# Thirty-six projection columns in pairs of seven block products, with the weight sums made by accumulating transfers

## What is computed

```python
proj = jnp.einsum("bld,de->ble", h, w_in)
conv_in, z_c, u_s, z_s, g_c, g_s = jnp.split(proj, IN_OFFSETS, axis=-1)
ca, cb = jnp.split(conv_in, 2, axis=-1)
cu = causal_depthwise_conv(ca * jax.nn.sigmoid(cb), conv_w, conv_b)      # 31 taps
cu = jax.nn.silu(layer_norm(cu, conv_ln_g, conv_ln_b))
conv_out = jnp.einsum("blc,cd->bld", cu * jax.nn.silu(z_c), w_conv_out)
y = jax.nn.gelu(s5_mimo(u_s, ...))
y = y * jax.nn.sigmoid(jnp.einsum("blc,ce->ble", y, w_glu) + b_glu)
ssm_out = jnp.einsum("blc,cd->bld", y * jax.nn.silu(z_s), w_ssm_out)
merged = jax.nn.sigmoid(g_c) * conv_out + jax.nn.sigmoid(g_s) * ssm_out
out = jnp.einsum("bld,de->ble", merged, w_out)
```

## Time and profile before

| | us |
|---|---|
| median of 3 runs | 2224.04 (2223.0 to 2225.08) |
| profiled execution, its own time | 2223.35 |
| its span, first to last instruction | 2221.6 |
| outside the span | 1.75 |
| granted TensorE clock, mean | 0.994 |

### The profile page before, as it was taken

How to read it: one execution, slowest core, us unless ns; L and a number is a source line. 1 busy time by engine, 2 the same in 40 slices (tenths; PEclk the granted TensorE clock), 3 DMA queues, 4 the chain that set the end, 5 groups by cost and what they waited for, 6 DMA issues and landing times. The chain is left out here.

```text
span 2221.6 us, 20647 instructions
## 1 busy us (share of the span) xinstructions
PE 2144.1 (97%) x7074; PEld 1093.5 (49%) x7074; DVE 1319.3 (59%) x1860; ACT 596.5 (27%) x972; POOL 185.2 (8%) x140
## 2 busy tenths in 40 slices
PE   6999999999999999998999999999999999999998
PEld 5444444445655655655454455544444444444443
DVE  4787733364674674664723695377468888335533
ACT  4355522233333433433213320021100000221011
POOL 0000000121212302301100000000000000003200
PEclk8999999999999999999999999999999999999999
DMA  9333330121111111111410334321111110113021
GB/s 331 116 110 118 118 123 0 76 65 38 35 30 43 35 26 47 35 25 48 125 31 19 124 66 68 87 63 33 43 33 43 38 33 24 52 48 123 19 95 57
DMA packets 200911, 146.86 MB, mean 66 GB/s; under 512 B 49997, under 2 KB 171906, under 8 KB 200834
## 3 DMA queue, kind: packets, MB, share of 16 engines
q1 hardware_dynamic: 184305, 143.09, 21.5%
q10 hardware_dynamic: 16160, 1.90, 0.8%
q0 software_dynamic: 384, 1.05, 0.2%
HBM read 126.45 MB, written 18.38 MB: 65 GB/s over the span
## 5 line engine op out<-in xcount | busy, mean ns | idle before, releaser
L2150 PE MATMUL bank<-hT,ring 128*128 128x512 f32 x1472 | 635.6, 593 | 0.0
L2150 PEld LDWEIGHTS bank<-hT,ring 128*128 128x128 f32 x1472 | 279.7, 190 | 348.6 <-issue 348.3
L1238 PE MATMUL bank<-hT,ring 128*128 128x512 f32 x336 | 157.8, 596 | 1.8 <-ACT silu_z L1474 1.8
L2870 DVE SCALAR_TENSOR_TENSOR yT<-s_arena,yT 128x1024 f32<-128x1024 f32 x120 | 153.3, 1278 | 0.0
L2870 DVE SCALAR_TENSOR_TENSOR s_arena<-s_arena 128x1024 f32<-128x1024 f32 x112 | 143.1, 1278 | 0.0
L1828 DVE SCALAR_TENSOR_TENSOR memory<-memory,col_exp_last,bank 128x128 f32<-128x128 f32 x64 | 22.2, 348 | 153.8 <-PE bank L1418 153.8
L2150 PE MATMUL bank<-ssm_y,ring 128*128 128x512 f32 x192 | 83.9, 593 | 0.0
L1238 PEld LDWEIGHTS bank<-hT,ring 128*128 128x128 f32 x336 | 58.5, 191 | 49.8 <-issue 49.4
L1238 PE MATMUL bank<-resid,yT 128*128 128x512 f32 x168 | 82.5, 594 | 0.0
L2853 DVE TENSOR_TENSOR s_arena<-bank,s_arena 128x1024 f32<-128x1024 f32 x8 | 9.8, 1224 | 108.7 <-ACT s_arena L2489 108.7
L2489 ACT ACTIVATE s_arena<-bank 128x1024 f32<-128x1024 f32 x8 | 8.2, 1024 | 242.5 <-PE bank L2150 242.5
(11 more groups left out here) (559 smaller groups left out, 3446.3 us busy)
## 6 DMA issues: line engine op xcount, KB each, us to landing
ring<-in_w_in SPq DMA_DIRECT2D x48, 512.0 KB, 3.8
ada<-in_ada_w SPq DMA_DIRECT2D x8, 2048.0 KB, 8.3
ring<-in_gdn_in_w SPq DMA_DIRECT2D x32, 512.0 KB, 4.1
resid<-in_x SPq DMA_DIRECT2D x8, 1024.0 KB, 8.8
ring<-in_lru_in_w SPq DMA_DIRECT2D x16, 512.0 KB, 3.9
lru_arena<-in_ada_w SPq DMA_DIRECT2D x6, 1024.0 KB, 13.0
x_scratch<-resid SPq DMA_DIRECT2D x2, 2048.0 KB, 10.6
decayT<-g_scratch SPq DMA_DIRECT2D x8, 512.0 KB, 4.3
```

The source lines that it names most:

```text
L1238: last = nc.tensor.matmul(bank[:, to, :], w[:, k, :], v[:, k, :], start=(first and k == 0), stop=(k == KB - 1), skip_group_check=not only)
L2150: last = nc.tensor.matmul(bank[:, 2 * PAIR[name] + h, :], w[:, k, :], src[:, k, h * HALF:(h + 1) * HALF], start=(k == 0), stop=(k == kt - 1))
L2870: dve_b.mark(dve.scalar_tensor_tensor(out=acc, in0=padded[:, p, j:j + S], scalar=taps[:, p, j:j + 1], in1=acc, op0=ALU.mult, op1=ALU.add), ...
```

## The change

The 36 columns a, b (16), zs (4), gs (8) and gc (8) of w_in are now computed two at a time, in 18 pairs: `ab0`..`ab7` join a{n} with b{n}, `zs0`, `zs1`, `gs0`..`gs3` and `gc0`..`gc3` join column n of a group with the one half a group further. For a pair, the weights form 2 x 2 blocks (512 input features by one column) and h forms 2 x 2 blocks `h11 h12 h21 h22` (512 features by 512 positions). Seven products P1..P7 of four source products each replace eight. Four sums of h (`h_T1`..`h_T4`) are made once by VectorE; for each pair, four sums of weights `U1`..`U4` are read from DRAM. Those sums are made during the first block on POOL's queue: a plain copy DRAM to DRAM, then accumulating transfers onto it. `silu_zc` no longer stays in `resid`, since `h_T1`..`h_T3` take its place: ACT stores each column to DRAM, and POOL loads it back later. `zc6` and `zc7` move ahead, around `y1`. The order of ACT and VectorE after `y1` is written out anew.

POOL, in the first block (ab sums are 2 MB each, gs and gc 1 MB, zs 0.5 MB):

```diff
+                    def copy_U(group, u):
+                        block = {"U1": (1, 0), "U2": (0, 0), "U3": (0, 0), "U4": (0, 1)}[u]
+                        g.dma_start(w_sums[group, u], w_block(group, *block)).then_inc(U_copied[group], 16)
+                    def add_U1_U3(group):
+                        g.wait_ge(U_copied[group], 4 * 16)
+                        g.dma_start(w_sums[group, "U1"], w_block(group, 1, 1), accum_op=ALU.add, max_dma_last_dim=4096).then_inc(U13_summed[group], 16)
+                        g.dma_start(w_sums[group, "U3"], w_block(group, 1, 0), accum_op=ALU.add, max_dma_last_dim=4096).then_inc(U13_summed[group], 16)
+                    def add_U2(group):
+                        g.wait_ge(U13_summed[group], 2 * 16)
+                        g.dma_start(w_sums[group, "U2"], w_sums[group, "U1"], accum_op=ALU.add, ...).then_inc(U2_summed[group], 16)
+                    def add_U4(group):
+                        g.wait_ge(U2_summed[group], 16)
+                        g.dma_start(w_sums[group, "U4"], w_sums[group, "U2"], accum_op=ALU.add, ...).then_inc(U4_summed[group], 16)
                     for n in range(KT):
                         if n >= 2:
                             pe_a.wait(g, f"gates{n - 2}")
                         g.dma_start(gw[:, n % 2, :, :], ...).then_inc(gw_loaded[n % 2], 16)
+                        # n = 2: copy ab U1, U2; 3: copy ab U3, U4; 4: add_U1_U3(ab); 5: add_U2(ab), copy gs U1, U2; 6: add_U4(ab), copy gs U3, U4
+                    add_U1_U3("gs")
+                    for u in ("U1", "U2", "U3", "U4"):
+                        copy_U("zs", u)
+                    add_U2("gs")
+                    add_U1_U3("zs")
+                    for u in ("U1", "U2", "U3", "U4"):
+                        copy_U("gc", u)
+                    add_U4("gs")
+                    add_U2("zs")
+                    add_U1_U3("gc")
+                    add_U4("zs")
+                    add_U2("gc")
+                    add_U4("gc")
```

```diff
+            PAIR_ORDER = ["ab0", "ab1", "zs0", "ab2", "zs1", "ab3", "ab4", "ab5", "gs0", "ab6", "gs1", "ab7", "gs2", "gs3", "gc0", "gc1", "gc2", "gc3"]
+            PAIR_BANKS = {name: ((0, 1, 6), (2, 3, 7))[n % 2] for n, name in enumerate(PAIR_ORDER)}
+            SINGLE_AFTER = {"ab3": ["glu0", "glu1", "glu2", "glu3"], "gs0": ["ssm0"], "ab6": ["ssm4"], "ab7": ["ssm1"], "gs2": ["ssm5"],
+                            "gs3": ["ssm2", "ssm6", "ssm3", "ssm7"]}
...
+                    def product(name, q, start, alone, src):
+                        block_done(f"{name}_{q}")
+                        for k in range(HK):
+                            last = nc.tensor.matmul(bank[:, to, :], w[:, k, :], src[:, k, :], start=(start and k == 0), stop=(k == HK - 1), ...)
+                    # a pair: P1 h11, P5 h_T1, wait kept0, P6 h_T2, P2 h21, wait kept1, P7 h_T3, wait kept2, P3 h22, wait kept3, P4 h_T4
...
                     finish(early("zc5"))
-                    finish(early("zs0"))
+                    finish(early("zc6"))
                     dve_b.wait(pe, "s1")
                     read_out(1)
+                    finish(early("zc7"))
...
                         act_b.mark(act.activation(silu_zc[:, n, :], pair(PAIR[f"zc{n}"]), ACT.Silu), f"zc{n}")
+                        act_b.wait(act, f"zc{n}")
+                        act.dma_start(zc_dram[n], silu_zc[:, n, :]).then_inc(zc_kept if n < 6 else zc_kept_late, 16)
...
+                    for group in W_GROUPS:
+                        sp.wait_ge(U4_summed[group], 16)
+                    for x in W_BLOCKS[8:]:
+                        pe_b.wait(sp, W_AT[x][2])        # the block eight places earlier has been used
+                        load_block(x)
+                    for n in (3, 0, 1, 2):
                         load(f"co{n}", a["w_conv_out_2"][0], n)
```

```diff
+                    dve.wait_ge(zc_kept, 6 * 16)
+                    # h_T1 = h11 - h12, h_T3 = h22 - h12, h_T2 = -h_T1 - h22, after zc7 on PE: h_T4 = -h_T2 - h21 (each 128 x 2048)
+                    def join_quarter(name, which, to, kept, product):
+                        dve_b.mark(TT_(place, other, place, ALU.add), f"{name}_" + ("C11", "C12", None, "C22")[which])
+                    join_columns("ab0")
...
+                    # col 0: taps 1-15, join ab1, taps 16-30          col 1: taps 1-3, join zs0, taps 4-23, join ab2, rest
+                    # col 2: taps 1-8, join zs1, taps 9-27, join ab3  col 3: taps; then glu 0-3 and z 0-3
+                    # join ab4; col 4: taps 1-14, join ab5, rest      col 5: 1-2, join gs0, 3-8, merge 0, 9-26, join ab6, rest
+                    # col 6: 1, merge 4, 2-16, join gs1, rest         join ab7; col 7: 1-5, merge 1, 6-24, join gs2, rest; merge 5, join gs3
...
+                    pe_b.wait(g, "ssm7")
+                    dve_b.wait(g, f"sq_total{KT - 1}")
+                    for k in range(KT):
+                        if k >= 5:
+                            dve_b.wait(g, f"y{k - 5}")
+                        g.dma_start(zc_places[k % 5], zc_dram[k]).then_inc(zc_back[k % 5], 16)
```

More of the change, by code:

```diff
@@ L1945, in block_program @@
             SLOT = {}
-            for names, slot in (
-                (["u0", "zc0", "zc2", "zc4", "zs0", "zs2", "zc6", "b2", "a3", "a4", "a5", "a6", "a7", "gc0", "gc4", "co0", "co4"], 0),
-                (["u1", "zc1", "zc3", "zc5", "zs1", "zs3", "a2"] + [f"ssm{n}" for n in range(KT)] + ["gc1", "gc5", "co1", "co5"], 1),
-                (["u2", "a0", "a1", "glu0", "glu2", "zc7", "b3", "b4", "b5", "b6", "b7", "gc2", "gc6", "co2", "co6"], 2),
-                (["u3", "b0", "b1", "glu1", "glu3"] + [f"gs{n}" for n in range(KT)] + ["gc3", "gc7", "co3", "co7"], 3),
-            ):
+            for names, slot in ((["u0", "zc0", "zc2", "zc4", "zc6", "co0", "co4"], 0), (["u1", "zc1", "zc3", "zc5", "zc7", "co1", "co5"], 1),
+                                (["u2", "co2", "co6"], 2), (["u3", "co3", "co7"], 3)):
                 for n, name in enumerate(names):
                     SLOT[name] = (slot, q0 + n + 1, names[n - 1] if n else None)
+            for n in range(4):
+                SLOT[f"co{n}"] = SLOT[f"co{n}"][:2] + (LAST_IN_SLOT[n],)
             for n, freed in enumerate(("co_P3_0", "co_P4_0", "co_P3_1", "co_P4_1")):
@@ L1962, in co_weights @@
                         "S2": co_S2, "S3": co_S3, "S4": co_S4}
-            QUICK = (["zs0", "b0", "zs1", "zs2", "b1", "zs3", "zc6"] + [f"glu{b}" for b in range(ST)] + ["b2", "zc7", "gs0", "ssm0"]
-                     + [f"{x}{n + d}" for n in range(3, KT) for x, d in (("b", 0), ("gs", -2), ("ssm", -2))]
-                     + [f"{x}{n}" for n in (KT - 2, KT - 1) for x in ("gs", "ssm")] + [f"gc{n}" for n in range(KT)])
-            EARLY = [f"u{b}" for b in range(ST)] + [f"zc{n}" for n in range(6)] + ["zs0"]
@@ new lines, in join_names, with tap_names, column_names @@
+            def join_names(name):
+                return [f"{name}_{x}" for x in ("C11", "C22", "C12")]
+            def tap_names(n, first, end):
+                return [f"t{n}_{j}" for j in range(first, end)]
+            def column_names(n, first, *parts):
+                names = list(first) + [f"taps{n}", f"cu{n}", f"t{n}_0"]
+                at = 1
+                for tap, then in parts:
+                    names += tap_names(n, at, tap) + list(then)
+                    at = tap
+                return names + tap_names(n, at, TAPS31) + [f"taps_done{n}", f"total{n}"]
@@ L1975, in block_program @@
-                         + [f"glu{b}" for b in range(ST)] + ["a2", "b2", "zc7", "gs0", "ssm0"]
-                         + [f"{x}{n + d}" for n in range(3, KT) for x, d in (("a", 0), ("b", 0), ("gs", -2), ("ssm", -2))]
-                         + [f"{x}{n}" for n in (KT - 2, KT - 1) for x in ("gs", "ssm")]
-                         + ["gc0", "sums"] + [f"gc{n}" for n in range(1, 5)] + ["squares"] + [f"gc{n}" for n in range(5, KT)]
+                                            "y0", "zc4", "w1", "zc5", "zc6", "y1", "zc7"]
@@ L2348, in _ @@
-                    for n in (KT - 2, KT - 1):
-                        quick(f"gs{n}", hT)
-                        quick(f"ssm{n}", ssm_y, ST)
-                    quick("gc0", hT)
+                    finish(early("zc7"))
+                    act_b.wait(pe, "zc6")
+                    two_columns("ab0", banks_free=False)
+                    act_b.wait(pe, "zc7")
+                    two_columns("ab1", banks_free=False)
+                    two_columns("zs0")
+                    two_columns("ab2")
@@ new lines, in _ @@
+                    two_columns("ab4", banks_free=False)
+                    two_columns("ab5")
+                    two_columns("gs0")
+                    act_b.wait(pe, "glu3")
+                    dve_b.wait(pe, f"z{ST - 1}")
+                    single("ssm0")
+                    two_columns("ab6")
+                    dve_b.wait(pe, "merge0")
+                    single("ssm4")
+                    two_columns("gs1")
```

(15 more changed lines are left out.)

653 lines of the change are left out of this document (471 added, 182 removed), and 3 rows, old and new, of the table dve_b.

## The result

The changed kernel takes 2210.57 us, the median of 4 runs (2206.01 to 2213.01), beside 2224.19 for the kernel before in the same series (4 runs, 2223.0 to 2225.08). The ratio is 0.9937, with a 95% interval from 0.9919 to 0.9954: faster by 0.6%, and not by the 2.4% that were forecast. 2210.57 lies above the range of 2161 to 2193. The profiled execution took 2206.01 us, its span is 2204.3.

What follows compares the result with a forecast made beforehand. PE's own work was taken to set the end from 1427.08 to 2021.25 us. Against 2223.35, -61.8 + 1.2 + 6 + 2.5 = -52.1 gave 2171 us; range 2161 to 2193.

Steps and rivals of the forecast that it cites:

- Part 1: Pairs after y1: 28 source products instead of 32 each, -61.8 us on PE, and +1.2 for waits at new products.
- Part 2: VectorE keeps up with the added sums and joins between y1 and co: cost 0, total7 8.9 us before sums is due.
- Rivals 1 and 4: VectorE becomes the bound, 2180 to 2195, chance 0.17; the products don't get shorter, 2232, chance 0.02.
- Part 3: Weight sums on POOL in the first block: +6 us at the first chunk, 0 for later copies and accumulations.
- Later in the loop the cover is thick: First block's loop: the chunk asked for at 153.08 is used at 175.42 and takes 8.3, so 14 us are free.
- rival 3: Accumulation is slow, POOL still waits for sums at 412.61 and the delta-rule block starts late; chance 0.11.
- the slow bound: Accumulating transfers at 99 GB/s, half of a store's 198; POOL's sums would then end near 356 us.
- The term for the first chunk: At n = 2, POOL's two copies delay SP's chunk and so PE one for one: +6 us, bounds 0 and +13.4.
- all 6.8 MB must pass before the chunk is whole: Upper bound at the first chunk: copies and loads all pass before it is complete, +13.4 us.
- half shares: Case at the first chunk where POOL's copies and SP's loads share the DMA engines equally: +8.4 us.
- Part 4: Stores of silu_zc while u_blk comes back: PE's wait there grows from 1.5 to 4 us, +2.5.
- rival 2: POOL's copies in the first block cost nothing: 2165 us, chance 0.10 more.

Runs made afterwards that it cites:

- the experiment on the second half: Changed kernel with SP's load of the out projection's second half issued before the loads of x, w_ab, dt_bias and neg_a; 2202.89 us, ratio 0.9925.

## Why the prediction was wrong

**Part 1** was right. y1 to `co`: 532.36 us for 533.6 forecast. PE never waits in it.

**Part 2** was right. VectorE kept up; `total7` ended 392.4 us after y1 (1863.96) where the working had 397.3, so its margin at `sums` was 12.9 us and not 8.9. Rivals 1 and 4 did not occur.

**Part 3** was wrong, and above all in one step: "Later in the loop the cover is thick", with the value 0. Of the transfers after the first two copies the working looked at one chunk in the loop and at the meeting. It passed over the loads that SP makes behind the loop (and the half columns of weights in it), although put POOL's free time, and so the sums, from 229 us on beside them. The out projection's first half has little cover: in the kernel before it is asked for at 266.49, lands after 7.7 us, and PE uses it at 279.88, 5.7 us later. POOL's additions of gs and all transfers of zs and gc run from 243 to 345 us; they cost 22.6 us at the first half and 9.0 behind it, in all 31.6. 1.4 us more are in the loop. Only SP's loads were missing in the working; that POOL would be idle long before the meeting was right (122.97 us), and rival 3 was wrong in its mechanism, though the block did start late as it said. The rate of an addition was not the problem either: 211 GB/s, twice the 99 that were taken as the slow bound. (The working counted 9.5 MB of additions behind the last `gw`; the code has 10.5, since the last addition of gs, 1.05 MB, is missing in it. At 99 GB/s POOL would still have been done some 45 us before 412.)

The working expected the wait for the chunk to grow from 7.3 to some 13 us; it grew to 19.80. The term for the first chunk had the right mechanism and was too small: +6 forecast, 13.4 measured, of which 12.5 are the wait, near the bound for "all 6.8 MB must pass before the chunk is whole". Two premises did not hold. The copies did not start behind the loads: POOL issued them from 73.51 us on, SP the chunk at 74.14. And the queues did not get half shares of the bytes: with as many packets served from each, POOL moved 3.88 MB from 76 to 92 us and SP 1.90, so that the 2.6 MB of loads were done only when nearly all of the 4.2 MB of copies were. That it is packets that are shared evenly is read from these counts; no run was made to test it, and it does not hold for the packets of 14 KB in the run with plain copies. That transfers of all queues run on the same 16 engines and interleave, which the Trainium skill says ("DMA: Bandwidth & Descriptors", section "Issuing engines are not separate DMA queues"), the runs bear out. The other page named in the prediction ("Collectives: The Full Stack", section "Why ReduceScatter is half of AllGather") would have an addition at half of a copy's rate, as it finds for transfers between cores; here it is 211 of 311 GB/s, 0.68. The measurement decides.

**Part 4**: PE's wait at u_blk is 3.28 us (forecast 4, before 1.53), the term +2.5 forecast, +1.7 between the two profiled executions, about 3 by the experiment. Right.

So the sum was short of 31.6 + 1.4 for the later transfers and 7.4 for the first chunk, 40.4 us. The rest is small: the profiled execution was 1.6 us earlier at the first group, the delta-rule block 2.1 shorter, parts 1 and 4 came out 1.2 and 0.8 better. 2171.25 + 40.4 - 5.7 = 2205.95, for 2206.01 measured.

Without the sums in the way, the forecast's own parts 1, 2 and 4 give 2165 (rival 2's figure); the kernel without sums took 2161.9, the one with the sums in idle stretches 2164.38.

The version with late stores takes 2161.46, ratio 0.9718 to the kernel before; against the changed kernel's 0.9937 that is 2.2% less.

## What to carry to other kernels

Before a bulk transfer is added on an idle queue, list every load of every other queue that will run beside it, up to its last byte, and look for each at how long the data lay before use. Where that is a few us, as the 5.7 of the out projection here, the load is nearly on the path, and what it is late beyond those us is waited for: it landed 28.2 us later after being asked, and PE's wait grew by 22.6. The end of a loop is the place to look at first, since the next stage's weights are asked for there. Look also at how long the packets of the two queues are, since the one with the longer packets took more of the engines here. A stretch with a DMA share of 0.00 was 60 us away; moving the 38 MB into it and into a second stretch where nobody waited turned a gain of 14 us into one of 60.

## What the runs showed of the hardware

- Beside POOL's bulk transfers a load of 2 MB took 35.9 us to land instead of 7.7, and SP needed 29.70 us to issue four loads of x instead of 2.45: contention holds up the issuing queue too (28.26 to 29.70 us in the three executions with the transfers behind the loop at the change's places, 11.73 with copies for the additions, 2.37 to 2.92 where no sum transfer stood beside it), and so the loads behind in it, which the experiment on the second half shows (5.4 us).
- While both queues had work, as many packets of the one as of the other were served, though POOL's were the longer ones: 2231 and 2233 from 280 to 315 us, with 7.08 and 2.70 MB; the kernel before with sums has 2342 and 2339 in the same stretch. This holds for packets of up to 4 KB; beside POOL's packets of 14 KB, in the run with plain copies, SP had 371 served for 89.
- DRAM to DRAM, copies run at 311 GB/s and additions at 211, with the engines full in both cases.
- A wait of PE costs more than its length: behind 23.32 us at the out projection the granted clock was still low, and 64 instructions took 1.9 us more.
- Not settled: the delta-rule block takes 778.7 to 779.1 us in all seven profiled executions in which ab sums run in the first block's loop, and 780.45 to 780.98 in the four in which none do. No run was made to find out why. The first column of the table, which varies by 8 us, goes in step with the granted clock from 40 to 60 us: 1.00 in the three executions that start it at 72.3 to 72.4, 0.97 in the three at 73.9 to 74.0, 0.93 at 75.5 and 75.6, 0.85 at 77.2 and 77.3, 0.76 at 80.6. Why the clock differs from one execution to the next is not known.
